# Two blocks on one core: a read-back and the last projection tile in halves, an earlier wait before the input transposes, and outputs turned between filter transposes

## What is computed

```python
h = rms_norm(x, pre_norm_w)
proj = h @ w_in                                   # 1024 -> 7168
hy_in, hy_gate, sg_u, sg_v, sg_gate = split(proj)
x0, x1, v = split(short_conv_centred(hy_in))      # three taps along the sequence
k = hyena_filter(...)                             # three sine layers, then a decayed long filter, divided by its L1 norm
y_a = x0 * long_conv_bidir(v * x1, k, skip) * silu(hy_gate)
mixed = einsum('hpq,bnqhd->bnphd', sgu_w, normed(sg_v)) + sgu_b
y_b = sg_u * mixed * silu(sg_gate)
x = x + rms_norm(concat([y_a, y_b]) @ w_out, post_norm_w)
```

## Time and profile before

| | us |
|---|---|
| median of 3 runs | 3129.09 (3126.72 to 3131.32) |
| the profiled execution, its own time | 3130.32 |
| span of its trace | 3128.5 |
| PE busy in the span | 2982.3 (95%) |
| DVE busy | 2531.5 (81%) |
| ACT busy | 827.0 (26%) |

### The profile page before, as it was taken

The page is one execution under the profiler, slowest core; times in us unless marked ns, Lnnn a source line. Parts: engine busy times, 40 slices in busy tenths (PEclk is TensorE's granted clock), DMA queues, the critical chain, the costliest instruction groups (busy, mean ns, idle before and its releaser), DMA issues. The chain is left out here.

```text
span 3128.5 us, 33046 instructions
## 1 busy us (share of the span) xinstructions
PE 2982.3 (95%) x12866; PEld 2163.7 (69%) x12866; DVE 2531.5 (81%) x2789; ACT 827.0 (26%) x1402; POOL 336.1 (11%) x458
## 2 busy tenths in 40 slices
PE   8999999999998999999999999999899989889999
PEld 4444444656777887888888888887656656678887
DVE  7979999898996869999999999998477979762221
ACT  3000000696334320000011111112343735631111
POOL 2211121001333430000000000000000100000000
PEclk9999999999999999999999999999999999989999
DMA  7675553201457546565554454541222331454331
GB/s 214 180 172 158 174 151 79 115 1 65 148 186 241 145 134 171 150 182 141 153 140 139 122 152 135 141 141 34 109 86 81 110 120 42 148 168 124 92 108 41
DMA packets 212115, 406.39 MB, mean 130 GB/s; under 512 B 21008, under 2 KB 134328, under 8 KB 204088
## 3 DMA queue, kind: packets, MB, share of 16 engines
q1 hardware_dynamic: 189256, 324.58, 34.2%
q0 software_dynamic: 21552, 71.32, 8.4%
q10 hardware_dynamic: 1152, 8.39, 0.7%
HBM read 324.53 MB, written 85.98 MB: 131 GB/s over the span
## 5 line engine op out<-in xcount | busy, mean ns | idle before, releaser
L1845 PE MATMUL PS<-HX,WH 128*128 128x512 f32 x1536 | 599.4, 390 | 6.9 <-DVE MB L1743 5.0
L1847 PE MATMUL PS<-HX,WL 128*128 128x512 f32 x1536 | 598.3, 390 | 0.0
L1846 PE MATMUL PS<-HX,WH 128*128 128x512 f32 x1536 | 598.3, 390 | 0.0
L849 PE MATMUL PS<-M 128*128 128x512 f32 x1088 | 472.0, 596 | 7.5 <-DVE M L650 6.3
L849 PEld LDWEIGHTS PS<-M 128*128 128x128 f32 x1088 | 207.4, 191 | 271.9 <-issue 263.7
L1845 PEld LDWEIGHTS PS<-HX,WH 128*128 128x128 f32 x1536 | 288.9, 188 | 67.9 <-DVE MB L1743 5.9
L1846 PEld LDWEIGHTS PS<-HX,WH 128*128 128x128 f32 x1536 | 288.9, 188 | 59.9
L1847 PEld LDWEIGHTS PS<-HX,WL 128*128 128x128 f32 x1536 | 288.7, 188 | 60.0
L120 DVE SCALAR_TENSOR_TENSOR HP<-MF,HP 128x1024 f32<-128x1024 f32 x252 | 323.5, 1284 | 8.0
L120 DVE SCALAR_TENSOR_TENSOR M<-M 128x1024 f32<-128x1024 f32 x160 | 205.6, 1285 | 26.5 <-DMA M<-c_feat 20.9
L2532 PE MATMUL PS<-WH,YH 128*128 128x512 f32 x512 | 202.1, 395 | 8.9 <-DVE HP L2671 5.2
(11 more groups left out here) (224 smaller groups left out, 5060.7 us busy)
## 6 DMA issues: line engine op xcount, KB each, us to landing
MF<-h_scratch SPq DMA_DIRECT2D x380, 256.0 KB, 4.3
M<-c_feat POOLq DMA_DIRECT2D x186, 256.0 KB, 4.4
MF<-w_in SPq DMA_DIRECT2D x52, 512.0 KB, 4.8
M<-u_scratch SPq DMA_DIRECT2D x16, 1024.0 KB, 4.9
M<-c_decay POOLq DMA_DIRECT2D x48, 256.0 KB, 2.9
M<-x SPq DMA_DIRECT2D x18, 512.0 KB, 4.1
M<-w_in SPq DMA_DIRECT2D x18, 512.0 KB, 5.9
x_scratch<-M SPq DMA_DIRECT2D x16, 512.0 KB, 5.0
```

The costliest lines, as they stand in the source:

```text
L849: ins = t.matmul(ps[:, c, :], wt[:, k], HT[:, k, TC * c:TC * c + TC], start=(k == 0), stop=(k == KD - 1))
L1845: t.matmul(dst, wh, hh, start=(k == 0), stop=False)
L1846: t.matmul(dst, wh, hl, start=False, stop=False)
L1847: ins = t.matmul(dst, wl, hh, start=False, stop=(k == KD - 1))
```

## The change

1. The read-back of VN is issued as two DMAs of eight token tiles each, with a semaphore for each half. The first eight matmuls of a `mix` tile wait for the first half, the other eight for the second.
2. The tile `("v", 7)` signals after two banks and again after four; ACT, the two tap passes and the product run on halves of 1024 columns. The store stays whole.
3. `inputs_turn` of an odd group waits for three of the even group's four transposes; the fourth is waited for ahead of the second step of `inputs_first`, which writes banks 2 and 3.
4. The first group's two output transposes are no longer together behind filter transpose 7: one stands behind transpose 5, the other behind transpose 10.

The diff, cut to its core:

```diff
@@ POOL, projection
-                    g.dma_start(VN[h % 2], vnr[h]).then_inc(vn_in, 16)
+                    for half in range(2):
+                        g.dma_start(VN[h % 2][:, 8 * half:8 * half + 8], vnr[h][:, 8 * half:8 * half + 8]).then_inc(vn_in[half], 16)
@@ ACT, projection
-                    if kind not in ("u", "mix"):
+                    if kind not in ("u", "mix") and (kind, n) != LAST_TILE:
                         s.wait_ge(tile_done, j + 1)
...
+                    elif (kind, n) == LAST_TILE:
+                        w = CW[:, 8 * CONV.index(kind) + n]
+                        s.wait_ge(gx_stored, 16 * (n + 1))
+                        for half in range(2):
+                            s.wait_ge(last_half_done, half + 1)
+                            part = slice(1024 * half, 1024 * half + 1024)
+                            s.activation(AB[0][:, part], ps[:, part], ACT.Identity, bias=w[:, 3:4], scale=w[:, 1:2]).then_inc(last_evac, 1)
@@ PE, projection
-                        t.wait_ge(vn_in, 16 * (n + 1))
                         for i in range(NT):
+                            if i % 8 == 0:
+                                t.wait_ge(vn_in[i // 8], 16 * (n + 1))
...
+                            if (kind, n) == LAST_TILE and c % 2:
+                                ins.then_inc(last_half_done, 1)
@@ DVE, long convolution
-                    filter_turned(cc + 1, range(2, 8))
-                outputs_turned(2 * cc)
-                if cc + 1 < NCH:
-                    filter_turned(cc + 1, range(8, 16))
+                    filter_turned(cc + 1, range(2, 6))
+                    outputs_turned(2 * cc, (0,))
+                    filter_turned(cc + 1, range(6, 11))
+                    outputs_turned(2 * cc, (1,))
+                    filter_turned(cc + 1, range(11, 16))
@@ PE, inputs_turn
-                    t.wait_ge(ut_done, 4 * ug)
+                    t.wait_ge(ut_done, 4 * ug - 1)
@@ PE, inputs_first
                     if g >= 2:
                         t.wait_ge(ut_done, n - 1)
+                    elif g == 1 and ug % 2:
+                        t.wait_ge(ut_done, 4 * ug)
```

More of the change, by code:

```diff
@@ L1590, in second_inputs @@
             sgt_in = [stage_sem("sgt_in%d" % i) for i in range(2)]
-            vn_in = stage_sem("vn_in")
+            vn_in = [stage_sem("vn_in%d" % i) for i in range(2)]
             mix_gated = stage_sem("mix_gated")
@@ L1603, in second_inputs @@
             sin3_done = stage_sem("sin3_done")
+            last_half_done = stage_sem("last_half_done")
+            last_evac = stage_sem("last_evac")
+            last_tap = stage_sem("last_tap")
+            LAST_TILE = ("v", 7)
             CONV = ("x0", "x1", "v")
@@ L1745, in outer_taps, with last_tile @@
                     v.wait_ge(taps_done, conv + 1)
+                def last_tile(ps, w):
+                    dst = AB[0]
+                    for half, (lo, hi) in enumerate(((0, 1023), (1023, S))):
+                        first, end = 1024 * half, 1024 * half + 1024
+                        v.wait_ge(last_evac, half + 1)
+                        v.scalar_tensor_tensor(out=dst[:, max(first, 1):end], in0=ps[:, max(first, 1) - 1:end - 1], scalar=w[:, 0:1],
+                                               in1=dst[:, max(first, 1):end], op0=ALU.mult, op1=ALU.add).then_inc(last_tap, 1)
+                        v.wait_ge(last_tap, 2 * half + 1)
+                        stop = min(hi, S - 1)
+                        v.scalar_tensor_tensor(out=dst[:, lo:stop], in0=ps[:, lo + 1:stop + 1], scalar=w[:, 2:3],
+                                               in1=dst[:, lo:stop], op0=ALU.mult, op1=ALU.add).then_inc(last_tap, 1)
+                        v.wait_ge(last_tap, 2 * half + 2)
+                        ins = v.tensor_tensor(AB[1][:, lo:hi], dst[:, lo:hi], AB[1][:, lo:hi], ALU.mult)
+                    ins.then_inc(u_done, 1)
                 def second_angle():
@@ L1780, in _ @@
                         v.tensor_tensor(AB[n % 2], ps, AB[n % 2], ALU.mult).then_inc(mix_gated, 1)
+                    elif (kind, n) == LAST_TILE:
+                        last_tile(ps, CW[:, 8 * CONV.index(kind) + n])
                     elif kind in CONV:
@@ L1847, in _ @@
                                 ins = t.matmul(dst, wl, hh, start=False, stop=(k == KD - 1))
-                    ins.then_inc(tile_done, 1)
+                            if (kind, n) == LAST_TILE and c % 2:
+                                ins.then_inc(last_half_done, 1)
+                    if (kind, n) != LAST_TILE:
+                        ins.then_inc(tile_done, 1)
             first_ctx.close()
@@ L2203, in inputs_turned, with outputs_turned @@
                                 PS[:, 2 * (g % 2):2 * (g % 2) + 2, :].rearrange("p x (c i) -> p c x i", i=16)).then_inc(ut_done, 1)
-            def outputs_turned(ug):
+            def outputs_turned(ug, halves=(0, 1)):
                 cc, ct = ug // 2, ug % 2
                 v.wait_ge(z_done, 16 * cc + 16)
-                for h in range(2):
+                for h in halves:
                     c = P * ct + 64 * h
```

## The result

The changed kernel takes 3111.5 us (median of 20 runs, 3102.2 to 3128.4) against 3131.0 of the kernel before (20 runs, 3123.6 to 3136.1). The ratio of the runs is 0.9949, with a 95% interval of 0.9936 to 0.9962: some 16 us are gone, and on the 3129.1 us of the prediction that is 3113.1. The two medians lie 19.5 us apart; the ratio takes in the longer runs of the changed kernel, which its median leaves out. It is faster by more than 0.2%, as was held most likely, but 11 us above the forecast of 3102 and just outside the range, which ended at 3113. The profiled execution took 3110.8 us, its span 3109.0.

A forecast was written before the change was run, and what follows sets the result against it. PE was taken to set the pace, with DVE only some 2 us behind. Savings of 9.5 + 4.2 + 6.4 + 7.1 = 27.2 us off 3130.3 gave 3103.1, or 3102 at the median's level; range 3097 to 3113.

The forecast's parts named there:

- The read-back in halves: Projection, odd heads' `mix` tiles: PE's waits for VN shrink and the clock stays up; 9.5 us saved.
- The even tiles: `mix` tiles of even heads show no clock fall, so waits left of about 1.6 us or less should cause none.
- d: Delay of VN's second half landing against the whole read: taken as 0.7 us, bounds 0 and 2.9.
- The last tile in halves: End of the projection: less ACT, tap and product work left behind the last matmul; 4.2 us saved.
- The wait for three of four: Odd input transposes start one even-group transpose earlier, 1.6 us at each of four waits; 6.4 us saved.
- The outputs between filter transposes: Filter passage between chunks: 2.35 us saved in each of three if the clock stays up; 7.1 us.
- The stepping: Filter passage walked transpose by transpose: 16.7 us in the new order, 17.4 in the old without a clock fall.
- the first of the two values: Saving in three filter passages at full clock, 7.1 us, chosen over 2.1 with the clock fall.
- The rival with a chance of 0.18: Clock falls in the filter passage all the same: 2.1 us saved in place of 7.1, time 3106.9; chance 0.18.
- the clock of the mix tiles: Three odd-head `mix` tiles run at half clock after their wait; full clock saves 1.7 us each, 5.1 us.
- the fixed part paid twice: VN read-back: each half pays the fixed DMA cost, delay 2.9 us, time 3110.7 to 3115.8; chance 0.12.
- halves that land together: VN read-back: the queue serves both halves side by side, that edit gives about 0, time 3111.4; chance 0.05.

The follow-up runs named there:

- the filled kernels: Idle matmuls, results unread, put in PE's waits: changed kernel 3103.1 and 3101.1 us, with the output stage also 3096.6; kernel before 3124.6.
- a longer run: Changed kernel repeated without edit, its trace taken in a slow execution: 3121.7 us at a mean clock of 0.983.
- run 15: No run number: the text reads "a longer run", then "15 us" lost; the run is the changed kernel repeated without edit, 3121.7 us.
- two fillers: Kernel before with only the new output order, plus two idle matmuls of 0.43 us at each filter passage's end: 3124.7 us, ratio 0.9977.
- the clock is held in either order: Changed kernel with idle matmuls in its waits, 3101.1 us (0.9912), against the same with outputs together as before, 3103.6 us (0.9912).
- the clock held in both kernels: Idle matmuls in the long convolution's waits of the kernel before, 3124.6 us (0.9985), and of the changed kernel, 3101.1 us (0.9912).
- the one test of timing: Changed kernel with four idle matmuls of 0.43 us ahead of the first chunk, making later waits come 1.7 us later: 3109.9 us, ratio 0.9938.

## Why the prediction missed, step by step

**The read-back in halves: right in kind, size within its scatter.** 10.65 us in the two profiled executions, against 9.5. Over all traces, the filled kernels among them, the stretch from the first `u` product to the first tap of `x0` is 362.3 us on average in the six with the whole read (359.1 to 365.4) and 354.8 in the fourteen with halves (353.2 to 357.8): 7.5. The execution of before that was shown was one of the dear ones, with three mix tiles at half clock where the trace without the halves, 359.1, had one. In the six, 14 `mix` tiles ran at half clock; in the fourteen, 5. The even tiles were no ground for the clock staying up behind the waits that are left, as they do not wait at all; it mostly did stay up, and not always. The landings came near the forecast: over heads 1 to 7 of all traces, a first half lands 6.9 us after its issue on average (forecast 6.7), a second half 9.7 after the issue of the first, and a whole one 9.4, so d is some 0.3 us where 0.7 was taken. The Trainium skill's "DMA: Bandwidth & Descriptors", section "Anatomy of one DMA — SWDGE (gpsimd) path", had stood against this edit with a fixed cost of about 2 us for each DMA. Of a second such cost little shows here: the last byte lands 0.3 us later.

**The last tile in halves: right.** 4.1 of 4.2 us: 5.92 in all fourteen traces that have the edit, 10.03 to 10.04 in the six that do not.

**The wait for three of four: right by itself.** 24.14 to 22.46 and 37.25 to 35.58 where no fall comes, 1.67 each, 6.7 in all against 6.4. In the profiled execution two of the four lost 1.0 and 1.5 of it to falls. With this edit alone, the two stretches of 71.8 took back 3.1 of it.

**The outputs between filter transposes: the step that failed.** The stepping was good: 16.7 forecast, 16.47 measured at full clock; 17.4 for the old order without a fall, 17.4 measured. What failed is the sentence that took the first of the two values "since the waits of 0.35 and 0.9 us are well under the 1.44 behind which no fall shows". The waits came out at 0.59, 0.52 and 0.28, and falls follow them all the same, 1.0 to 1.5 us each and now and then 7.65. The rival with a chance of 0.18, that the clock falls in the passage all the same, had the right enemy and the wrong place: the passage stays up, the work behind it does not. Inside the three passages 6.9 of the 7.1 came in the profiled execution, but 3.3 were lost right around them (0.8 ahead of the first, 1.0 and 1.5 behind the later ones), at places where the run without the new order shows no fall. The 1.6 + 1.6 on the way to the next product stay in that run, so they are not this edit's. In a longer run 15 us are lost behind the passages. With only the new order the kernel is 5 us slower than before (1.0017) where 7.1 were to be gained, with two fillers in these waits 7.2 faster (0.9977), and where the clock is held in either order the edit is worth 2.7 by the traces and nothing that the times show.

**The sum.** With the clock held in both kernels, the traces are 3118.7 - 3098.6 = 20.1 us apart: 7.6 for the read-back, 4.1, 6.6, and 2.7 for the order make 21.0. The forecast of 27.2 had 5.1 for the clock of the mix tiles and 5.0 for that of the passages in it; the first came in part, the second was mostly lost again around the passages. Three slips of its arithmetic change nothing in this: with d = 2.0 the time is 3107.1 and not 3106.9, its best case is 3099.5, and the twice-paid part together with the clock of the passages gives 3120.8, below 3122.8.

**Chances and the range.** Two rivals that would have given the right time, 3110.7 to 3115.8 for the fixed part paid twice and 3111.4 for halves that land together, are both refuted by the landings, with a first half at 6.9 and a second at 9.7 us. The runs were taken to scatter by 2 us; the changed kernel's scatter by 26, and the range, made for one clock case in one place, was too narrow for that.

**What stays open:** why a given wait brings a fall in one execution and none in another, and why a fall behind the passage lasts 17 us in some and 3 in others. The traces show when, not why; the one test of timing was too small.

## What to carry to other kernels

A wait of TensorE costs its length and, sometimes, the clock behind it; a gain that counts on the clock staying up is counted only with a reason why no wait is left at all. Where short waits lie ahead of dense matmuls, idle matmuls into a free bank can be cheap insurance: here they brought 3105.8 to 3096.6 us on one chip, more than either of the two useful edits that ran alone (6.9 and 7.8 us); in the kernel before they gave 4.7. Judge an edit by the stretches of the trace that have no fall in them, and by many runs sorted by their mean granted clock; a pair of medians mixes both.

## What the runs showed of the hardware

- A fall of the granted clock follows waits as short as 0.28 to 0.59 us when several come close together; waits of 2.1 us go without one in other executions (1.17 and not 1.88 us for the four matmuls behind). The Trainium skill, "TensorE: Matmul & The Clock Gate", section "A second HAM failure mode: psum-queue depth-cycling", tells of a clock that swings because PE idles briefly, again and again, while it cycles through PSUM banks; the end of the filter passage is such a place, and the runs agree: with fillers in two of these waits the stretch behind it goes from 44.9 to 37.2 us.
- Once down, the clock can stay at 1.2 GHz for 17 us while PE is busy without a break: 16.00 of 16.00 us in the run with only the new order, at 0.50.
- The same kernel takes 3102 to 3129 us, and its times follow its mean granted clock, 0.991 to 0.980 (correlation -0.98 over 20 runs). The Trainium skill's same page, section "What's actually happening", says that the gate runs on by itself and does not start afresh with a kernel, so that the same kernel measures differently; that the times follow the mean clock agrees with it.
- Two DMAs of 512 KB on GpSimd's queue under load take hardly longer than one of 1 MB: on average the second half lands 9.7 us after the first issue (98 read-backs), the whole after 9.4 (42), and the first half is there after 6.9.
